# Output tiles inside the last attention group, and head weights spread on ScalarE, in a six-stage one-core kernel

## The reference

```python
wts = jax.nn.softmax(jnp.stack(lses, axis=0), axis=0)
o = jnp.sum(wts[..., None] * jnp.stack(outs, axis=0), axis=0)
o = o.reshape(Bsz, S, DIL_OUT) * jax.nn.silu(g.astype(jnp.float32))
mixed = jnp.concatenate([y.astype(jnp.float32), o], axis=-1).astype(x.dtype)
return x + jnp.einsum("bsf,fd->bsd", mixed, w_out.astype(x.dtype))
```

## Time and profile before

| | us |
|---|---|
| runs, median (lowest to highest) | 1834.65 (1826.57 to 1835.35) |
| the profiled execution's own time | 1835.43 |
| its span | 1833.3 |
| PE busy in it | 1632.1 (89%) |
| share of the span on the chain that ended last: PE, DMA | 73%, 17% |
| mean granted TensorE clock | 0.971 of full |
| stage SSD's last output matmuls, from / to | 1590.8 / 1639.4 |
| stage MOBA's last output matmuls, from / to | 1801.2 / 1829.1 |

### The profile page before, as it was taken

The page is one execution under the profiler, slowest core; times in us unless marked ns, Lnnn a source line. Parts: engine busy times, 40 slices in busy tenths (PEclk is TensorE's granted clock), DMA queues, the critical chain, the costliest instruction groups (busy, mean ns, idle before and its releaser), DMA issues.

```text
span 1833.3 us, 24382 instructions
## 1 busy us (share of the span) xinstructions
PE 1632.1 (89%) x10510; PEld 1011.0 (55%) x10510; DVE 357.4 (19%) x755; ACT 264.4 (14%) x654; POOL 112.3 (6%) x163
## 2 busy tenths in 40 slices
PE   8999988988897987989899889978989899889997
PEld 7855554555554774455555555547745544544554
DVE  1832000000002023320000000013332432230222
ACT  2011000000001023110000000011311322301330
POOL 0000000000000012000000000000003133003110
PEclk9999999999999998999999999998999899899999
DMA  9539999999999531299999999994422223133100
GB/s 401 205 125 425 427 428 428 428 429 429 429 429 428 223 138 46 90 428 426 429 429 428 429 428 428 429 428 187 155 92 80 86 92 132 53 138 132 52 1 23
DMA packets 36187, 504.64 MB, mean 275 GB/s; under 512 B 4000, under 2 KB 4128, under 8 KB 5792
## 3 DMA queue, kind: packets, MB, share of 16 engines
q1 hardware_dynamic: 34976, 499.60, 65.6%
q0 software_dynamic: 1152, 4.19, 0.6%
HBM read 502.73 MB, written 1.05 MB: 275 GB/s over the span
## 4 chain that ended last, share of the span: by engine, by line
PE 73%; DMA 17%; DVE 5%; ACT 2%; issue 2%; POOL 0%; SPq 0%; ACTq 0%; DVEq 0%
DMA ring<-in_expert_up 17%; PE ps L978 12%; PE ps L591 9%; PE ps L707 9%; PE ps L724 7%; PE ps L622 7%; PE ps L764 7%; PE ps L691 4%; PE ps L776 3%; PE ps L973 2%; PE ps L601 2%; PE ps L877 2%; PE ps L568 1%; PE ps L882 1%; PE ps L1030 1%
## 5 line engine op out<-in xcount | busy, mean ns | idle before, releaser
L707 PE MATMUL ps<-x_tok,constants_sb 128*128 128x256 f32 x1232 | 307.1, 392 | 0.0
L724 PE MATMUL ps<-ring,arena 128*32 128x256 f32 x3968 | 238.2, 382 | 55.9 <-DMA ring<-in_expert_up 53.7
L707 PEld LDWEIGHTS ps<-x_tok,constants_sb 128*128 128x128 f32 x1232 | 221.4, 189 | 105.2 <-issue 81.3
L978 PE MATMUL ps<-ring,spare 128*128 128x512 f32 x480 | 214.0, 601 | 2.0 <-ACT arena L1391 1.3
L724 PEld LDWEIGHTS ps<-ring,arena 128*32 128x32 f32 x3968 | 121.6, 109 | 163.4 <-DMA ring<-in_expert_up 44.4
L591 PE MATMUL ps<-spare,ring 128*128 128x256 f32 x704 | 158.4, 389 | 2.5 <-DMA ring<-in_stream 1.7
L978 PEld LDWEIGHTS ps<-ring,spare 128*128 128x128 f32 x480 | 90.1, 192 | 111.6 <-issue 108.5
L591 PEld LDWEIGHTS ps<-spare,ring 128*128 128x128 f32 x704 | 137.6, 196 | 22.8 <-DVE spare L1571 3.1
L622 PE MATMUL ps<-ring,arena 128*128 128x512 f32 x288 | 126.9, 599 | 0.5 <-ACT arena L1376 0.5
L764 PE MATMUL ps<-ring,arena 128*32 128x512 f32 x960 | 115.0, 597 | 13.3 <-ACT arena L1283 13.3
L1764 DVE TENSOR_TENSOR arena<-arena,ps 128x128 f32<-128x128 f32 x64 | 18.4, 288 | 521.2 <-ACT arena L1288 521.2
(11 more groups left out here) (263 smaller groups left out, 1368.1 us busy)
## 6 DMA issues: line engine op xcount, KB each, us to landing
ring<-in_expert_up SPq DMA_DIRECT2D x124, 2048.0 KB, 24.7
ring<-in_expert_down SPq DMA_DIRECT2D x60, 2048.0 KB, 27.1
ring<-in_stream SPq DMA_DIRECT2D x44, 2048.0 KB, 8.5
arena<-in_expert_up SPq DMA_DIRECT2D x4, 2048.0 KB, 14.5
arena<-in_expert_down SPq DMA_DIRECT2D x2, 2048.0 KB, 21.9
spare<-in_expert_down SPq DMA_DIRECT2D x2, 2048.0 KB, 18.9
constants_sb<-in_constants SPq DMA_DIRECT2D x1, 1766.0 KB, 18.1
x_tok<-in_x SPq DMA_DIRECT2D x1, 1024.0 KB, 5.5
```

The source lines that it names most:

```text
L707: pe.matmul(ps[:, b, 0:TOK], ident, x[:, 0, 0:TOK], start=True, stop=True, skip_group_check=True)
L724: ins = pe.matmul(ps[q * SLOTS:(q + 1) * SLOTS, 4 + e % 2, 0:TOK] .rearrange("p (g n) -> p g n", g=2), xg[:, 4 * half + k, e * SLOTS:(e + ...
L978: ins = pe.matmul(bank(b + part), xT[:, k, part * P:(part + 1) * P], w[:, k, :], start=(k == 0), stop=(k == KT - 1))
```

## The change

1. `weights_T` now does 8 transposes of 128x128 (`pe.transpose`) instead of 16 matmuls. Their input `at_wx` (two buffers of 128x1024 in `arena` from word 4096, a place that the squares, the rotation's products and `ss_z` have left by then) holds each weight repeated 64 times along the free axis.
2. ACT makes it: `spread(grp)` is one Copy of 128x1024 with a broadcast input, counted by the new semaphore `at_wx`, on which PE waits ahead of each `weights_T`. SSD: spreads 0 and 1 after `at_weighed`, spread 2 after the first `weights_T` (its buffer is spread 0's). MOBA: spread 0 after ACT's copy at pair 0 of the last group, spread 1 after all of ACT's attention.
3. SSD: the t = 0 tiles of output chunks 0 and 1 become the fills of pairs 2 and 3 of the last group. After the attention follow chunk 0 tile 1; `weights_T(0)`, `weights_T(1)`; the first 512 columns of chunk 1 tile 1; `weights_T(2)`; the other 512 columns; the wait for `at_mixT`; chunk 2.
4. MOBA: the t = 0 tile of chunk 0 becomes the fill of pair 3, after a wait for `at_mixT` of group 0. After the attention: `weights_T(1)`; chunk 0 tile 1; wait; chunk 1.
5. DVE in MOBA: `mixed(0)` moves ahead to pair 2 of the last group, behind its copy of the probabilities (`move_pT(2)`) and ahead of `masked(3)`. `between` gets the pair as argument for that.

```diff
+        at_wx = [arena[:, 4096 + n * D:4096 + (n + 1) * D].rearrange("p (t c) -> p t c", t=2)
+                 for n in range(2)]
...
             def weights_T(grp, b):
+                spreads[0] += 1
+                pe.wait_ge(sem("at_wx"), spreads[0])
                 for pr in range(4):
                     for t in range(2):
-                        for hh in range(2):
-                            h, c = 2 * pr + hh, (pr % 2) * TOK + t * P
-                            ins = pe.matmul(ps[64 * hh:64 * hh + 64, b + pr // 2, c:c + P],
-                                            at_wt[:, grp, t, h:h + 1].broadcast_to([P, 64]),
-                                            ident, start=True, stop=True, skip_group_check=True)
+                        c = (pr % 2) * TOK + t * P
+                        ins = pe.transpose(ps[:, b + pr // 2, c:c + P],
+                                           at_wx[grp % 2][:, t, pr * P:(pr + 1) * P], ident)
...
-                attention(2, [("gate", g + 15)])
-                pe.wait_ge(sem("at_proj"), projected[0])
-                output(g + 16, 3, mixT12, None, before=before)
+                def early(c):
+                    pe.wait_ge(sem("at_proj"), projected[0])
+                    output_tile(g + 16, 3, mixT12, None, c, 0)
+                attention(2, [("gate", g + 15)], [lambda: early(0), lambda: early(1)])
+                output_tile(g + 16, 3, mixT12, None, 0, 1)
+                pe.wait_ge(sem("at_weighed"), 1)
+                pe.wait_ge(sem("at_o_moved"), 6)
+                pe.wait_ge(sem("at_pT_moved"), 24)
+                weights_T(0, 4)
+                weights_T(1, 6)
+                output_tile(g + 16, 3, mixT12, None, 1, 1, parts=(0,))
+                pe.wait_ge(sem("at_wT_used"), 1)
+                weights_T(2, 4)
+                output_tile(g + 16, 3, mixT12, None, 1, 1, parts=(1,))
+                pe.wait_ge(sem("at_mixT"), 1)
+                output(g + 16, 3, mixT12, None, 2)
...
+                def early():
+                    pe.wait_ge(sem("at_mixT"), no + 1)
+                    output_tile(g + 8, 2, mixT12, None, 0, 0)
-                attention(g_no(4), [("gate", g + 7)], [first_weights])
+                attention(g_no(4), [("gate", g + 7)], [first_weights, early])
                 weights_T(1, 4)
+                output_tile(g + 8, 2, mixT12, None, 0, 1)
+                pe.wait_ge(sem("at_mixT"), no + 2)
+                output(g + 8, 2, mixT12, None, 1)
...
+            def spread(grp):
+                act.activation(at_wx[grp % 2].rearrange("p t (h d) -> p (t h) d", d=64),
+                               at_wt[:, grp].rearrange("p t h -> p (t h)").unsqueeze(2)
+                               .broadcast_to([P, 16, 64]), ACT.Copy).then_inc(sem("at_wx"), 1)
...
-                attention(n + 1, 1, causal, False, last=lambda: (mixed(0), reciprocals(1)))
+                attention(n + 1, 1, causal, False, lambda pr: mixed(0) if pr == 2 else None,
+                          lambda: reciprocals(1))
```

More of the change, by code:

```diff
@@ L610, in residual, with output_tile @@
                                   start=True, stop=False, skip_group_check=True)
-            def output_tile(g0, n_chunks, mixT, scale, c, t, seeded=False):
+            def output_tile(g0, n_chunks, mixT, scale, c, t, seeded=False, parts=(0, 1)):
                 if c == 0 and scale is not None and not seeded:
@@ L619, in output_tile @@
                 w = slot4[slot(g0 + c)]
-                for n in range(2):
+                for n in parts:
                     for k in range(4):
@@ L626, in output_tile @@
                                         skip_group_check=True)
-                if t == 1:
+                if t == 1 and n == 1:
                     ins.then_inc(chunk_done, 1)
-                elif c == n_chunks - 1:
+                elif t == 0 and c == n_chunks - 1:
                     ins.then_inc(tile_out, 1)
@@ L981, in half @@
                     ins.then_inc(chunk_done, 1)
+            spreads = [0]
             def weights_T(grp, b):
+                spreads[0] += 1
+                pe.wait_ge(sem("at_wx"), spreads[0])
                 for pr in range(4):
                     for t in range(2):
-                        for hh in range(2):
-                            h, c = 2 * pr + hh, (pr % 2) * TOK + t * P
-                            ins = pe.matmul(ps[64 * hh:64 * hh + 64, b + pr // 2, c:c + P],
-                                            at_wt[:, grp, t, h:h + 1].broadcast_to([P, 64]),
-                                            ident, start=True, stop=True, skip_group_check=True)
+                        c = (pr % 2) * TOK + t * P
+                        ins = pe.transpose(ps[:, b + pr // 2, c:c + P],
+                                           at_wx[grp % 2][:, t, pr * P:(pr + 1) * P], ident)
                 ins.then_inc(sem("at_wT"), 1)
@@ L1528, in ssd_dilated @@
                 act.activation(at_em, at_em, ACT.Exp).then_inc(sem("at_em_exp"), 1)
+                act.wait_ge(sem("at_weighed"), 1)
+                spread(0)
+                spread(1)
+                act.wait_ge(sem("at_wT"), 1)
+                spread(2)
             def block_attention():
@@ L1541, in block_attention, with first_spread @@
                 attention(n, 0, [(kind, g + 4 + c) for c, kind in enumerate("qkv")])
-                attention(n + 1, 1, [("gate6", g + 7)])
+                no = 1 if SSD in on else 0
+                def first_spread(pr):
+                    if pr == 0:
+                        act.wait_ge(sem("at_weighed"), no + 1)
+                        spread(0)
+                attention(n + 1, 1, [("gate6", g + 7)], first_spread)
+                act.wait_ge(sem("at_weighed"), no + 2)
+                spread(1)
             if first != CONV:
@@ L1913, in mean_squares, with attention @@
                     .then_inc(sem("head_v"), 1)
-            def attention(grp, out_g, mask, qk_ahead, between=lambda: None, last=lambda: None):
+            def attention(grp, out_g, mask, qk_ahead, between=lambda pr: None,
+                          last=lambda: None):
                 move_T(qk_turn(grp), at_qkT)
@@ L1952, in attention @@
                 move_pT(1)
-                between()
+                between(1)
                 masked(2)
@@ L1957, in attention @@
                 move_pT(2)
+                between(2)
                 masked(3)
@@ L2050, in ssd_dilated, with between @@
                 dve.sem_inc(sem("ss_y_taken"), 1)
[L2052 to L2055, removed]
+                def between(pr):
+                    if pr == 1:
+                        dve.wait_ge(sem("ss_sq"), 8)
+                        inv_root(ss_ss, ss_ss, 1.0 / 256, RMS_EPS)
+                        dve.sem_inc(sem("ss_rstd"), 1)
                 add4 = C("att_add").rearrange("p (n c) -> p n c", n=4)
```

## The result

The changed kernel takes 1817.62 us, the median of 8 runs (1812.83 to 1823.23); the kernel before, run beside it, 1829.08 (8 runs, 1825.83 to 1835.35). The ratio is 0.9932 with a 95% interval of 0.9908 to 0.9955. In a second set, 6 runs on another chip beside 11 of before, it was 0.9907 (0.9885 to 0.9929). That is 12.4 us (8.2 to 16.8) and 17.0 us (13.0 to 21.0) of 1830; the forecast was 17.2. The profiled execution of the changed kernel took 1812.93 us, span 1810.8.

What follows compares the result with a forecast made beforehand. PE's own stream was taken to bound the late stages. SSD's 12.8 plus MOBA's 4.4 made 17.2 us off the profiled 1835.43, 1818.2; that execution stood 0.8 above the median, so 1817.5, range 1808.5 to 1825.5.

Steps and rivals of the forecast that it cites:

- SSD, 12.8 us: SSD's last group and output: 6.8 us of waits, 2.7 of weights_T, about 4 of half clock, less 0.5.
- A: Stretch from mix(1) in SSD's last group, or the tile there, to SSD's last output record; forecast gain 12.8 us.
- both softmax waits: SSD's last group: PE's waits of 3.41 and 3.35 us for ACT's exponentials would go, covered by tile and mix.
- 0.65 left ahead of `mix(3)`: SSD's last group: mix(3) would still wait 0.65 us for the copy of pair 3's probabilities.
- the 0.5 reckoned: SSD's output: chunk 2 would start 0.5 us late, DVE needing 3.9 us after weights_T(2), the half tile covering 3.5.
- The step sum: The forecast's step-by-step gains, 12.8 us in SSD and 4.4 in MOBA, 17.2 in all; weights_T in SSD counted 2.7.
- MOBA, 4.4 us: MOBA's last group and output: chunk 1 would end at 1824.6 against 1829.05, a gain of 4.4 us.
- no fall of the clock: MOBA's last group: clock stays up through two gaps of some 2.5 us, at 7 to 3; a fall costs up to 3.4.
- B: Stretch in MOBA from the start of the first weights_T to the end of the last output record; forecast gain 4.4 us.
- Nothing is won: MOBA's weights_T(0): 1.0 us instead of 1.80 gains nothing, as PE waits for the exponentials until 1787.54 all the same.
- Rival 1: Clock falls anyway, behind SSD's three weights_T (1.7 us) and in MOBA (3.4 us): gain 12.1, 1822.5 us; chance 0.12.
- Rivals 2 to 4: MOBA gains nothing, 1822 (0.08); ACT's broadcast copy slow, 1841 (0.02); idle time reappears, gain about 5, 1830 (0.04).

Runs made afterwards that it cites:

- Order only: The changed kernel's new order in both stages, but with the old 16 matmuls per weights_T and no spreads: 1818.08 us, ratio 0.9922 to the kernel before.
- MOBA-only kernel: The change in MOBA alone, SSD with the old order, old matmuls and no spreads: 1828.40 us, ratio 0.9980 to the kernel before.
- SSD-only kernel: The change in SSD alone, MOBA with the old order, old matmuls and no spreads: 1817.92 us, ratio 0.9936 to the kernel before.

## Why the prediction was right

- **SSD, 12.8 us.** Measured 13.1 in A (50.8 us, against 63.9 in the profiles with the old SSD code), and 50.8 in all six profiles with SSD's changed code and single spreads. The steps held one by one: both softmax waits gone, 0.65 left ahead of `mix(3)`, a wait of 0.47 before chunk 2 for the 0.5 reckoned (3.9 less 3.5 would have made it 0.4), spreads hidden. `weights_T` was a little dear at 1.0 each; three took 1594.68 to 1596.43 and 0.87, that is 2.6.
- **What it is made of.** Order only leaves 3.1 to the transposes in A and 10.0 to the order. The step sum had 2.7 for them.
- **MOBA, 4.4 us.** Measured 4.5 (6.0 against the other profile of MOBA's old code), with the same row order as forecast: `early` released by DVE's second product, nothing ahead of pair 3's transposes, 0.47 ahead of the last `weights_T`. But one step of it failed: I took no fall of the clock there, at 7 to 3, and it fell in every profile with the new `weights_T(0)` as the fill of pair 2 (pair 2's transposes slow in six of six), never with the old one (three of three). It cost little in the changed kernel, since the tile waits for `mixed(0)` anyway: transposes and scores took 1.4 us longer, the wait behind them was 1.45 instead of 2.7, and the tile started 8.86 us after B's start, for 8.64 reckoned. In the MOBA-only kernel it cost 3 more.
- **"Nothing is won" by the first `weights_T`.** That was too kind. The 0.8 us saved beside a wait lengthened the wait from 1.67 to 2.39, and the longer one goes with the fall. Whether the length of the wait or the kind of instruction (transposes for matmuls) does it, these runs don't separate.
- **Transposes and the clock.** The Trainium skill, page "TensorE: Matmul & The Clock Gate", section "Part 4: PE-mode transpose", says that the full clock does not engage for transposes. The traces don't bear that out as it stands. In the kernel before, the clock went from 0.50 to 1.00 behind sixteen transposes and nothing else on PE. In the changed kernel the same sixteen were followed by 5 us more at half, but in A, with the 24 transposes of three `weights_T`, the clock is 1.00 throughout:

```profile
1568.00:1618.80 50.80, 49.68 (x166) 23.68 (x164) 16.43 (x25) 11.45 (x26) 0.00 (x0) 1.00 0.30 117
```

- **The sum against the clock on the wall.** 17.2 lies just above the first interval (8.2 to 16.8 us) and in the middle of the second (13.0 to 21.0). The forecast did not have the 2.6 at MOBA's start; with it the stretches give 15.0, inside both. Rival 1 named a fall of the clock as the thing that could eat the gain, and priced it at 5 us; 2.6 came, at MOBA's start, a place that it did not name. Rivals 2 to 4 are refuted by B = 41.3, by 1.05 us per spread and by A.
- **The level.** The median of before was 1834.65 in the three runs that I had and 1829.08 in eight, so the starting point was 5.6 us too high. The gain by these medians is 11.5, 5.7 less than the 17.2 of the forecast. The two cancel: that 1817.5 met 1817.62 is luck, and what speaks for the mechanism is A and B.

## What to carry to other kernels

Put work that is independent of a softmax into the wait for it, sized so that tile plus neighbours exceed the latency of the chain (here 7.9 us, and with half tiles 4.4, for 4.3). It was worth the waits that it filled plus the half clock that came with them (10.0 us of A from the order alone). When that work has itself a late input, move that input's producer ahead first (here `weights_T(0)` and `mixed(0)`, with the tile cut in halves: 6.7 us of stretch B). Shortening work that lies beside a wait won nothing here: the wait grew by nearly all that was saved. Before believing a difference of a few microseconds between two profiles, cut both into stretches and see whether the ones with equal code agree.

## What the runs showed of the hardware that I had not expected

- A stretch of unchanged code repeated to 0.02 us from execution to execution (A 50.81 to 50.83, six profiles); in the two of these whose stretches were read, the clock was at 1.00 throughout. Other stretches do not repeat: from the last matmul group of the mixture of experts to A's start, with the same code, it took 340.5 to 340.6 us in three profiles, 343.3 in one and 346.7 to 347.5 in five. In the three PE was busy for 302 us at a mean granted clock of 0.95, in the five for 309 to 310 us at 0.93. That is up to 7 us of the spread of 8 to 10 us between runs.
- The same 96 records of 128x512 took 41.47 or 43.87 us by how long half clock lasted after the same wait of 4.75; in the SSD-only kernel and in the changed kernel even with the same instructions ahead.
- In the two kernels with useless matmuls at SSD's start, the first of them came 3.73 and 3.53 us after PE's last work, and the profile names no releaser. Between the two PE's stream has a wait for `m_counted`, a load of the token count into a register and a conditional block that is skipped; which of these takes the time is not shown.
